# Loading V of expert row n and U of row n + 1 in one transfer of 8 KB per partition

## The reference

```python
def one_block(xb):                      # 128 tokens
    ...                                 # two sets of 128 sub-keys, top 16 of each, top 16 of their sums
    idx = e1 * N_KEYS + e2              # 8 heads x 16 experts per token, of 128 x 128
    gate = jax.nn.softmax(best, axis=-1)
    u_sel = expert_u[idx]
    act = jax.nn.gelu(jnp.einsum('bqhkd,bqd->bqhk', u_sel, xb), approximate=False)
    w = (gate * act).astype(xb.dtype)
    return jnp.einsum('bqhk,bqhkd->bqd', w, expert_v[idx])
```

## Time and profile before

| | |
|---|---|
| runs shown | 1726.26 us median, 1724.62 to 1731.73 |
| the profiled execution | 1727.33 us, its span 1725.0 us |
| TensorE matmul busy | 1622.8 us, 94% |
| VectorE busy | 1184.2 us, 69% |
| GpSimd busy | 883.3 us, 51% |
| DMA: gathers' queue | 73728 packets, 268.47 MB, 39.7% of 16 engines |
| DMA: SP's queue | 65280 packets, 219.85 MB, 35.0% of 16 engines |
| chain that ended last | DMA 40%, PE 33%, DVE 12%, POOL 7%, issue 5% |

### The profile page before, as it was taken

One profiled execution on the slowest core, in us unless ns is written; L12 is line 12 of the kernel. 1 busy time (PEld: TensorE's weight loads), 2 busy tenths in 40 slices (PEclk: granted clock), 3 DMA queues, 4 the chain that ended last, 5 costly groups with the idle time before them and its releaser, 6 DMA issues.

```text
span 1725.0 us, 20488 instructions
## 1 busy us (share of the span) xinstructions
PE 1622.8 (94%) x6590; PEld 1159.5 (67%) x6590; DVE 1184.2 (69%) x2625; ACT 342.8 (20%) x783; POOL 883.3 (51%) x1117
## 2 busy tenths in 40 slices
PE   7989999999899989987799999999999999999997
PEld 5768887686687658876366666666666666666664
DVE  4656488569664559799766766766666666667666
ACT  3244331212343112388000000001000000000001
POOL 6756566348653337600745544545654455445442
PEclk9999999999999989999899999999999999999999
DMA  6422235344897964200999999999999999999997
GB/s 211 122 74 74 68 122 153 113 156 135 295 323 273 352 219 135 85 0 9 399 409 409 409 409 409 409 409 409 408 409 403 408 409 408 409 409 407 409 408 270
DMA packets 139100, 489.47 MB, mean 284 GB/s; under 512 B 16497, under 2 KB 17009, under 8 KB 138881
## 3 DMA queue, kind: packets, MB, share of 16 engines
q0 software_dynamic: 73728, 268.47, 39.7%
q1 hardware_dynamic: 65280, 219.85, 35.0%
HBM read 483.53 MB, written 4.72 MB: 283 GB/s over the span
## 4 chain that ended last, share of the span: by engine, by line
DMA 40%; PE 33%; DVE 12%; POOL 7%; issue 5%; ACT 2%; SPq 1%; DVEq 0%; POOLq 0%; ACTq 0%
DMA ring<-in_expert_v,chosen 23%; DMA ring<-in_expert_rows,chosen 16%; PE pair L723 15%; PE pair L735 4%; POOL ring L692 4%; DVE ring L1476 4%; DVE ring L1473 3%; PE pair L1029 2%; PE pair L770 1%; DVE temp L1712 1%; PE pair L756 1%; PE pair L1013 1%; PE pair L816 1%; PE pair L793 1%; PE pair L971 1%
## 5 line engine op out<-in xcount | busy, mean ns | idle before, releaser
L692 POOL DMA_INDIRECT ring<-in_expert_rows,chosen x256 | 286.5, 1119 | 359.8 <-DVE ring L1473 320.2
L1013 PE MATMUL pair<-temp,hnT 128*128 128x512 f32 x984 | 445.5, 595 | 25.8 <-DVE hnT L1352 21.8
L1476 DVE SCALAR_TENSOR_TENSOR ring<-ring,chosen 128x1024 f32<-128x1024 f32 x256 | 328.9, 1285 | 156.6 <-DMA ring<-in_expert_v,chosen 154.0
L1004 PE MATMUL pair<-hnT,temp 128*128 128x256 f32 x1904 | 430.4, 379 | 0.0
L1004 PEld LDWEIGHTS pair<-hnT,temp 128*128 128x128 f32 x1904 | 361.8, 190 | 100.0 <-issue 56.9
L1473 DVE SCALAR_TENSOR_TENSOR ring<-ring 128x1024 f32<-128x1024 f32 x256 | 311.1, 1224 | 131.2 <-DMA ring<-in_expert_rows,chosen 130.0
L692 POOL DMA_INDIRECT ring<-in_expert_v,chosen x256 | 266.7, 1042 | 251.2 <-DVE ring L1476 230.1
L1013 PEld LDWEIGHTS pair<-temp,hnT 128*128 128x128 f32 x984 | 182.9, 190 | 224.5 <-issue 213.8
L1326 ACT ACTIVATE hnT<-pair 128x256 f32<-128x256 f32 x119 | 45.7, 384 | 811.7 <-PE pair L1004 685.1
L723 PE MATMUL pair<-hnT,gate_all 128*128 128x256 f32 x592 | 135.3, 385 | 1.4 <-issue 1.4
L723 PEld LDWEIGHTS pair<-hnT,gate_all 128*128 128x128 f32 x592 | 112.6, 194 | 16.5 <-issue 1.7
(11 more groups left out here) (292 smaller groups left out, 1925.0 us busy)
## 6 DMA issues: line engine op xcount, KB each, us to landing
temp<-in_expert_v SPq DMA_DIRECT2D x128, 512.0 KB
temp<-in_expert_u SPq DMA_DIRECT2D x119, 512.0 KB
gate_all<-in_w_query SPq DMA_DIRECT2D x27, 512.0 KB
ring<-in_w_g SPq DMA_DIRECT2D x16, 512.0 KB, 3.5
gate_all<-in_w_g SPq DMA_DIRECT2D x11, 512.0 KB
gate_all<-in_expert_u SPq DMA_DIRECT2D x9, 512.0 KB
ring<-in_w_u SPq DMA_DIRECT2D x8, 512.0 KB, 4.1
ring<-in_w_k SPq DMA_DIRECT2D x8, 512.0 KB, 4.0
```

Of the source, the lines that this page charges most:

```text
L692: pool.indirect_dma_start(out=gathered[:, g % SLOTS, :], out_offset=None, in_=(expert_rows, expert_v_rows)[part], in_offset=bass.IndirectO ...
L1004: mm = pe.matmul(u_out[n % 2], u_in[:, n % 2, c * P:(c + 1) * P], hnT[:, c, FIRST[1]:L], start=(c == 0), stop=(c == DC - 1))
L1013: mm = pe.matmul(pairs[i][:, b * 512:(b + 1) * 512], weighed[n][:, i * P:(i + 1) * P], v_in[:, n % 2, b * 512:(b + 1) * 512], start=False, ...
L1476: dve.scalar_tensor_tensor(out=fin, in0=slot, scalar=wsel[:, at:at + 1], in1=fin, op0=ALU.mult, op1=ALU.add).then_inc(row_done, 1)
```

## The change

V of expert row n and U of row n + 1 stand side by side in one input tensor `expert_uv` (8 KB per partition; U is rolled by one row on the host) and come in one transfer. Two buffers of both, 8 KB per partition each, replace two buffers of each; one semaphore per buffer replaces two. The transfer of row n is issued once `v_part(n - 2)` is done. Rows 0 to 7 bring only V, since U up to row 8 was computed ahead, and so does row 127. The first transfers of the sweep are V of rows 0 and 1 alone; U of row 9 comes with V of row 8. `u_part(n)` waits for the transfer of row n - 1. The nine U rows loaded ahead are taken from the new tensor. The one-hot tiles are laid out over the same memory in another order, and the last residual goes to the U half of the second buffer.

```diff
@@ hybrid_program
-        u_in = temp[:, 0:2 * D].rearrange("p (s n) -> p s n", s=2)
-        v_in = temp[:, 2 * D:4 * D].rearrange("p (s n) -> p s n", s=2)
+        uv_in = temp[:, 0:4 * D].rearrange("p (s n) -> p s n", s=2)
+        v_in, u_in = uv_in[:, :, 0:D], uv_in[:, :, D:2 * D]
...
-        oh1 = v_in.rearrange("p s (b t e) -> p (s b) t e", b=2, t=4)
-        oh2 = [u_in[:, s, b * 512:(b + 1) * 512].rearrange("p (t e) -> p t e", t=4) for s in range(2) for b in range(2)]
+        oh1, oh2 = ([v[:, s, b * 512:(b + 1) * 512].rearrange("p (t e) -> p t e", t=4) for s in range(2) for b in range(2)]
+                    for v in (v_in, u_in))
...
-        u_landed = [sem(f"u_landed{i}") for i in range(2)]
-        v_landed = [sem(f"v_landed{i}") for i in range(2)]
+        uv_landed = [sem(f"uv_landed{i}") for i in range(2)]
...
-        loads3 = ... [(("ahead", n), expert_u[n], product(("ahead", n))) for n in range(AHEAD)]
+        loads3 = ... [(("ahead", n), expert_uv[(n - 1) % P][:, D:2 * D], product(("ahead", n))) for n in range(AHEAD)]
@@ block.sync
-            def load_u(n):
-                if n >= AHEAD + 2:
-                    sp.wait_ge(u_product, n - AHEAD - 1)
-                sp.dma_start(u_in[:, n % 2, :], expert_u[n]).then_inc(u_landed[n % 2], 16)
-
-            def load_v(n):
+            def load_rows(n):
                 if n >= 2:
                     sp.wait_ge(v_product, n - 1)
-                sp.dma_start(v_in[:, n % 2, :], expert_v[n]).then_inc(v_landed[n % 2], 16)
+                width = 2 * D if AHEAD <= n + 1 < P else D
+                sp.dma_start(uv_in[:, n % 2, 0:width], expert_uv[n][:, 0:width]).then_inc(uv_landed[n % 2], 16)
 
             sp.wait_ge(onehot_free, 4 + HALF // 4)
-            load_v(0)
-            load_v(1)
-            load_u(AHEAD)
-            load_u(AHEAD + 1)
+            load_rows(0)
+            load_rows(1)
             for n in range(P + 1):
-                if AHEAD + 2 <= n < P:
-                    load_u(n)
                 if n >= 3:
-                    load_v(n - 1)
+                    load_rows(n - 1)
...
-            sp.dma_start(u_in[:, 0, :], h1_dram[3]).then_inc(res_landed[3], 16)
+            sp.dma_start(u_in[:, 1, :], h1_dram[3]).then_inc(res_landed[3], 16)
@@ block.tensor
             def u_part(n):
-                pe.wait_ge(u_landed[n % 2], 16 * ((n - AHEAD) // 2 + 1))
+                pe.wait_ge(uv_landed[(n - 1) % 2], 16 * ((n - 1) // 2 + 1))
                 pe.wait_ge(gelu_done, n - 1)
                 for c in range(DC):
-                    mm = pe.matmul(u_out[n % 2], u_in[:, n % 2, c * P:(c + 1) * P],
+                    mm = pe.matmul(u_out[n % 2], u_in[:, (n - 1) % 2, c * P:(c + 1) * P],
                                    hnT[:, c, FIRST[1]:L], start=(c == 0), stop=(c == DC - 1))
                 mm.then_inc(u_product, 1)
 
             def v_part(n):
-                pe.wait_ge(v_landed[n % 2], 16 * (n // 2 + 1))
+                pe.wait_ge(uv_landed[n % 2], 16 * (n // 2 + 1))
@@ kernel
-        "expert_u": a["expert_u"].reshape(P, P, DC, P).transpose(0, 3, 2, 1).reshape(P, P, D),
+        "expert_uv": np.concatenate([a["expert_v"].reshape(P, P, D), np.roll(
+            a["expert_u"].reshape(P, P, DC, P).transpose(0, 3, 2, 1).reshape(P, P, D), -1, axis=0)], axis=2),
```

More of the change, by code:

```diff
@@ L117, in hybrid_program @@
                    w_gg, w_out, a_re, a_im, log_dt, b_re, b_im, c_re, c_im, d_skip, w_query, keys,
-                   expert_u, expert_rows, expert_v, out):
+                   expert_uv, expert_rows, expert_v, out):
     heads = [[(j, h) for j in TILES[hf] for h in range(HEADS)] for hf in range(2)]
@@ L419, in hybrid_program @@
         loads2 += branches(1, ("att", "val"))
-        loads3 = branches(1, ("gg",)) + projections("qry", w_query, 1) + [(("ahead", n), expert_u[n], product(("ahead", n))) for n in range(AHEAD)]
+        loads3 = branches(1, ("gg",)) + projections("qry", w_query, 1) + [(("ahead", n), expert_uv[(n - 1) % P][:, D:2 * D], product(("ahead", n))) for n in range(AHEAD)]
         slots1 = [ring[:, s, :] for s in range(NW1)]
@@ L548, in _ @@
             sp.wait_ge(u_product, P - AHEAD)
-            sp.dma_start(u_in[:, 0, :], h1_dram[3]).then_inc(res_landed[3], 16)
-            for i, src in ((1, fin), (2, xrow), (3, u_in[:, 0, :])):
+            sp.dma_start(u_in[:, 1, :], h1_dram[3]).then_inc(res_landed[3], 16)
+            for i, src in ((1, fin), (2, xrow), (3, u_in[:, 1, :])):
                 sp.wait_ge(out_ready, i + 1)
@@ L1029, in _ @@
                         mm = pe.matmul(pairs[2 + s // 2][:, (s % 2) * 512 + t * P:(s % 2) * 512 + (t + 1) * P],
-                                       oh2[s][:, t], oh1[:, s, t], start=True, stop=True)
+                                       oh2[s][:, t], oh1[s][:, t], start=True, stop=True)
                     mm.then_inc(onehot_free, 1)
@@ L1334, in _ @@
             final(1, fin, junk)
-            for i, src in ((2, xrow), (3, u_in[:, 0, :])):
+            for i, src in ((2, xrow), (3, u_in[:, 1, :])):
                 ac.wait_ge(h2_ready, i - 1)
@@ L1711, in _ @@
                         at = it * 16 + b * 4 + t
-                        ins = dve.tensor_scalar(oh1[:, b, t], iota[:], first_key[:, bass.ds(at, 1)],
+                        ins = dve.tensor_scalar(oh1[b][:, t], iota[:], first_key[:, bass.ds(at, 1)],
                                                 gate_chosen[:, bass.ds(at, 1)], ALU.is_equal, ALU.mult)
@@ L1736, in _ @@
                     final(0, fin)
-            ends = ((2, xrow), (3, u_in[:, 0, :]))
+            ends = ((2, xrow), (3, u_in[:, 1, :]))
             for i, h in ends:
```

## The result

The changed kernel takes 1790.66 us in the median of four runs (1787.2 to 1806.15); the kernel before took 1726.42 us beside it. The ratio is 1.0384, with a 95% interval of 1.0319 to 1.0449: 64 us slower, outside the forecast's range of 1713 to 1751 us and on the other side of its likeliest case. The profiled execution took 1792.16 us, its span is 1789.7 us.

The account below looks back on a forecast made before the run. The prediction took DMA throughput, through the gathers, VectorE and its product, as the bound. Its terms, -4.4 + 0 + 1 = -3.4 us against the profiled 1727.33 us, gave 1723.9 us, 1723 us as median; range 1713 to 1751 us.

Parts of the forecast that it names:

- likeliest case: Whole kernel: 1723 us, within 0.5% of the kernel before, chance 0.42; its own range 1718 to 1734 us.
- What bounds the kernel: Sweep over expert rows: DMA throughput at 408 GB/s sets the pace, through the gathers, VectorE and its product.
- the wait that moves: Joint load before u_part: one step for twice the bytes; counted at 0, ends 0 and +35 us.
- L: Time a joint 1 MB load lasts beside gathers: 6.34 us without backlog to 7.78 us with a full one.
- full backlog: Gathers queued ahead of a load, taken as 1.44 us of its 3.93 us fixed time.
- The formula for a step: Sweep step with two buffers: (L + 0.19 + 6.89) / 2, 6.71 us without backlog, 7.43 us with a full one.
- full-backlog bound: Upper end for the joint load's wait in the sweep: 119 x (7.43 - 7.14) = +35 us.
- Rival 2: At uv_landed ahead of u_part: the joint wait becomes the bound; +25 us, 1751 us; chance 0.28, with rival 3 included.
- The load's share of the engines: Load queue beside gathers: two thirds for 8 KB against 4 KB packets, 3.85 us for 1 MB; half for equal packets.
- Larger packets: Expert loads in the sweep: 8 KB packets save 4.6 ns per 8 KB, -4.4 us; bounds nothing to 21 us.
- The start: Sweep start: U rows 9 and 10 no longer fill the engines during first gathers; +1 us, 2.6 us at most.
- The 2 us a step: Expert loads: the skill page's fit gives 6.4 us for two halves, 4.4 us for one whole, favouring the change.

Follow-up runs that it names:

- the early U rows: The changed kernel with U of rows 9 and 10 loaded at the sweep's start in transfers of their own, as before the change: 1780.47 us.
- the two forms with three buffers: The changed kernel with a pieced-together third buffer from row 8 on: 1736.46 us with 8 KB transfers in two of three loads, 1743.24 us with all 4 KB.
- the 4 KB form: The changed kernel with V and U halves apart in SBUF, so its one 1 MB transfer is made of 4 KB pieces: 1861.42 us.

## Why the prediction was wrong

**What bounds the kernel** was read rightly: DMA through the gathers. With three buffers and the early U rows the same waits and the same 408 GB/s come back.

**The step that failed is the wait that moves**, and in it the sentence that the two meet at L = 7.12 us: "as soon as steps are longer than DMA needs, VectorE catches up with the gelu, rows stay in their slots, fewer gathers queue ahead of the load, and L falls. So I count this wait at 0". It cost some 50 us by the runs, 57 us by the steps. The first half happened: VectorE waits 249.9 us for the gelu. The second didn't. The loads issued from 900 to 1700 us took 7.9 us in the median and 7.7 us in the mean, as much as the 7.78 us I had for a full backlog, and those on the chain 8.3 us. The queue ahead of a load didn't shrink either: in the packet records, averaged over these loads, gathers move 0.65 MB in the first 2 us after the issue and the load 0.08 MB; the 1.44 us of backlog that I had called full are 0.59 MB. A step still makes three and a half gathers however late it is, and VectorE works them off in one go after the gelu and the product, as here:

```profile
1203.71 5.24 DVE L1467 SCALAR_TENSOR_TENSOR ring<-ring,chosen 128x1024 f32<-128x1024 f32 x4
```

Each row done lets GpSimd issue the next gather: one goes out at 1205.26 us, the load at 1206.31 us, and three more gathers by 1210.07 us. That a load is short with a quarter of the gathers is shown (4.9 us). That their bunching is what keeps it long was only read from the traces, and no run moved the gathers in time.

A second thing was missing from L altogether. A transfer reports its landing in 16 updates, and the joint wait needs the last. In the median the fourteenth came after 6.8 us, the fifteenth after 7.5 and the last after 7.9 us; in the kernel before, the fourteenth and the last of a 512 KB load came after 6.6 and 6.7 us. With 6.8 us the formula below gives 6.94 us a step, which would have cost nothing (an estimate).

The formula for a step has the right form. With the 8.3 us of the chain it gives (8.3 + 0.19 + 6.89) / 2 = 7.69 us against 7.62 us measured. But those are the loads that held TensorE up; with the 7.73 us that all of them took in the mean it gives 7.41 us, since it knows nothing of loads that come now early and now late. Fed with the forecast's own full-backlog bound it gave +35 us. So over half of the sweep's loss was priced as the end of a range and then argued away by a mechanism that no row of before showed. Rival 2 names place and mechanism; its price, +25 us, was too low for the same reason, since it took a load with no backlog at all.

**The load's share of the engines** was the better half of the working. I took two thirds for 8 KB pieces and half for equal ones. With 4 KB pieces my numbers for half the rate and a full backlog give L = 9.06 us, where the median is 9.0 us. They give steps of 8.07 us; there were 96 loads in 800 us, 8.33 us.

**Larger packets**, -4.4 us: the sign fits the comparison of the two forms with three buffers, and the size was too small, 3 us against 6.8 us. The term that was mis-sized is the 4.6 ns saved per 8 KB, which measured 12 ns there. In the changed kernel itself nothing was saved: the load queue's share is 37.6% for 112.50 MB after and 37.5% for 119.29 MB before, and a packet of 8 KB took 350 ns where two of 4 KB had taken 327 ns. Why packets stretch when loads come bunched stays open.

**The start**, +1 us with an upper end of 2.6 us, was some 10 us. I had bounded it by the bytes that no longer fill the engines, and counted the first U part's wait at 0 "while gathers go on". They don't for long: rows are tied to steps. TensorE's wait of 4.5 us, the 2.6 us that its slow U part lost after that and the gap in the gathers came to four times the bound.

**The sum by the runs**: 1790.66 - 1780.47 = 10 us for the start, 1780.47 - 1730.51 = 50 us for the window, and 4 us of the 64 left. Taken in the other order the third buffer is worth 1790.66 - 1736.46 = 54 us and the early U rows then 6 us, so the split is good to some 4 us. The 50 us hold both the longer waits and the small sizes above: the gain of larger packets and what the third buffer's 1 KB pieces cost, some 7 us each way.

The Trainium skill's rule of at least 1 MiB per transfer (page "DMA: Bandwidth & Descriptors", section "Rules for kernel authors") speaks for this change. The 2 us a step that the prediction estimated from that page's fit were not there to gain; the page gives the fit for transfers issued by GpSimd, and these are issued by SP. The runs disagree with the rule for a stream that is queued anyway: the merged loads made the kernel 64 us slower, and what decided was how early a transfer was issued before its use.

## What to carry to other kernels

Before merging two transfers, write down for each how long its buffer is free before the data is needed, and compare that with the landing time beside the other traffic, not alone. Merging takes the shorter of the two windows and gives it the bytes of both. When a forecast prices a new wait at nothing because "the queue will shrink", that step needs a row of its own, or the price stands at its bound; and when two buffers alternate, half of what each landing is late by is paid in every step. A transfer is as late as its last piece, so its landing is a spread and not one number.

## What was not expected of the hardware

**A load's last tenth.** The load issued at 1206.31 us was followed through the DMA queues from 1206.3 to 1208.3, 1208.3 to 1210.8 and 1210.8 to 1213.6 us (packets, MB, share of 16 engines):

```profile
q1 hardware_dynamic: 21, 0.17, 35.4%
...
q1 hardware_dynamic: 104, 0.77, 76.8%
q0 software_dynamic: 41, 0.16, 16.8%
...
q0 software_dynamic: 271, 1.00, 91.3%
q1 hardware_dynamic: 17, 0.10, 8.5%
```

For 2.5 us the load has three quarters of the engines and the gathers one sixth; I had assumed two thirds for the load. Then 0.10 MB take another 2.8 us, while the gathers have 91.3%, and TensorE starts only at 1214.70 us. The transfer counts as landed when its last piece is, so the bulk being early is of no use. Its sixteen landing updates say the same: fourteen came by 1211.87 us, the fifteenth at 1213.02 and the last at 1214.65 us. Which engines were behind, and why, the records don't say.

**Order alone was worth 132 us.** The same two transfers of 512 KB, issued 0.4 us apart, cost that much more with the wrong one first.

**This stall of TensorE cost more than its length.** After the wait of 4.53 us at row 8, 16 matmuls took 6.23 us in place of 3.62. The stretches from 864 to 869 us (the wait) and from 869.4 to 872 us (the start of the U part), with the granted clock as the third number from the end:

```profile
864.00:869.00 5.00, 0.89 (x3) 0.06 (x1) 3.27 (x6) 0.00 (x0) 4.04 (x4) 0.87 1.04 421
869.40:872.00 2.60, 2.58 (x6) 2.13 (x7) 0.00 (x0) 0.00 (x0) 0.80 (x1) 0.50 1.00 413
```

0.50 is the lower of the two levels, 1.2 GHz. TensorE had been busy for 0.89 of the 5 us before. The stall cost 2.6 us more than the wait shows, a term that my count of the start left out. In the sweep it is rare in the changed kernel (3 of 105 U parts took over 5 us) and frequent where the waits are longer (16 of 96 in the 4 KB form).
